# Products without a reader in two waits of TensorE: the first norm, and before the first output projection

## What is computed

```python
def rms_norm(x, g):
    xf = x.astype(jnp.float32)
    y = xf * lax.rsqrt(jnp.mean(xf * xf, axis=-1, keepdims=True) + EPS)
    return (y * g.astype(jnp.float32)).astype(x.dtype)
...
        x = x + mixers[i % N_MIXERS](rms_norm(x, norm_mix), *mix_params)
        x = x + sqrelu_mlp(rms_norm(x, norm_ffn), w1, w2)
```

## Time and profile before

| | us |
|---|---|
| median of 3 runs | 1702.68 |
| lowest, highest | 1695.72, 1703.55 |
| the profiled execution | 1700.87 |
| its span | 1698.8 |
| TensorE busy | 1627.7 (96%) |
| VectorE busy | 975.7 (57%) |
| ScalarE busy | 686.7 (40%) |
| mean granted clock of TensorE | 0.981 |

### The profile page before, as it was taken

The page is one execution under the profiler, slowest core; times in us unless marked ns, Lnnn a source line. Parts: engine busy times, 40 slices in busy tenths (PEclk is TensorE's granted clock), DMA queues, the critical chain, the costliest instruction groups (busy, mean ns, idle before and its releaser), DMA issues.

```text
span 1698.8 us, 24770 instructions
## 1 busy us (share of the span) xinstructions
PE 1627.7 (96%) x9418; PEld 1304.7 (77%) x9418; DVE 975.7 (57%) x1500; ACT 686.7 (40%) x1040; POOL 242.0 (14%) x222
## 2 busy tenths in 40 slices
PE   6999978999999999999799999999999999999998
PEld 3777757888888887667457888878787788888887
DVE  5555645444444457787466768586774544444443
ACT  6455543323232355424455445362543432323232
POOL 0234330000000033143200403104040000000000
PEclk7999989999999999999899999999999999999999
DMA  4222213333333334223103122131220333333333
GB/s 132 74 72 65 63 38 87 87 99 99 99 92 101 92 98 119 63 66 86 37 4 108 40 75 75 51 87 51 65 62 26 88 104 93 99 95 102 87 100 99
DMA packets 258158, 135.07 MB, mean 80 GB/s; under 512 B 10699, under 2 KB 254940, under 8 KB 258068
## 3 DMA queue, kind: packets, MB, share of 16 engines
q1 hardware_dynamic: 258068, 133.84, 28.1%
HBM read 131.64 MB, written 2.18 MB: 79 GB/s over the span
## 4 chain that ended last, share of the span: by engine, by line
PE 78%; DVE 9%; issue 7%; ACT 4%; POOL 1%; DMA 0%; DVEq 0%; POOLq 0%; PEldq 0%; ACTq 0%; SPq 0%; PEld 0%
PE bank L231 18%; PE bank L233 18%; PE bank L232 18%; PE bank L1680 4%; PE bank L493 3%; PE bank L495 3%; PE bank L494 3%; DVE arena L1985 2%; DVE w_lo L215 2%; ACT w_hi L211 1%; PE bank L1260 1%; PE bank L1514 1%; PE bank L1696 1%; PE bank L1733 1%; DVE arena L2127 1%
## 5 line engine op out<-in xcount | busy, mean ns | idle before, releaser
L211 ACT CAST w_hi<-raw 128x1024 fp32r<-128x1024 f32 x234 | 245.0, 1047 | 260.4 <-PE bank L233 237.3
L231 PE MATMUL bank<-m_hi,w_hi 128*128 128x512 f32 x856 | 337.5, 394 | 6.0 <-POOL w_lo L221 2.8
L233 PE MATMUL bank<-m_hi,w_lo 128*128 128x512 f32 x856 | 334.3, 391 | 0.0
L232 PE MATMUL bank<-m_lo,w_hi 128*128 128x512 f32 x856 | 334.3, 391 | 0.0
L215 DVE TENSOR_TENSOR w_lo<-raw,w_hi 128x1024 fp32r<-128x1024 f32 x218 | 271.2, 1244 | 102.4 <-ACT w_hi L211 100.6
L231 PE MATMUL bank<-h_hi,w_hi 128*128 128x512 f32 x640 | 256.2, 400 | 10.6 <-DVE w_lo L215 6.2
L232 PE MATMUL bank<-h_lo,w_hi 128*128 128x512 f32 x640 | 252.7, 395 | 0.0
L233 PE MATMUL bank<-h_hi,w_lo 128*128 128x512 f32 x640 | 252.4, 394 | 0.0
L231 PEld LDWEIGHTS bank<-m_hi,w_hi 128*128 128x128 f32 x856 | 161.5, 189 | 43.1 <-issue 5.5
L232 PEld LDWEIGHTS bank<-m_lo,w_hi 128*128 128x128 f32 x856 | 161.5, 189 | 34.4 <-issue 1.2
L233 PEld LDWEIGHTS bank<-m_hi,w_lo 128*128 128x128 f32 x856 | 161.4, 189 | 33.9
(11 more groups left out here) (282 smaller groups left out, 2264.4 us busy)
## 6 DMA issues: line engine op xcount, KB each, us to landing
raw<-in_l_w_ff SPq DMA_DIRECT2D x64, 512.0 KB, 4.0
raw<-in_w_in SPq DMA_DIRECT2D x64, 512.0 KB, 3.8
raw<-in_w_mlp_up SPq DMA_DIRECT2D x32, 512.0 KB, 4.0
raw<-in_w_mlp_down SPq DMA_DIRECT2D x32, 512.0 KB, 4.0
raw<-in_l_w_in SPq DMA_DIRECT2D x24, 512.0 KB, 3.8
raw<-in_l_w_out SPq DMA_DIRECT2D x8, 512.0 KB, 3.7
arena<-gb_rows SPq DMA_DIRECT2D x16, 256.0 KB, 4.7
raw<-in_w_out SPq DMA_DIRECT2D x8, 512.0 KB, 4.1
```

The source lines that it names most:

```text
L211: act.copy(w_hi[q.par][:], raw[q.par][:]).then_inc(s["w_hi_ready"], 1)
L231: pe.matmul(g_bank[q.par][:], w_hi[q.par][:, k], hi[:, k], start=(k == 0), stop=False)
L232: pe.matmul(g_bank[q.par][:], w_hi[q.par][:, k], lo[:, k], start=False, stop=False)
L233: last = pe.matmul(g_bank[q.par][:], w_lo[q.par][:, k], hi[:, k], start=False, stop=(k == KT - 1))
```

## The change

A helper issues n products into bank `b[5]`, whose results nothing reads. It is called in three places: five products ahead of the waits for `x_s` and `n_acc` in `pe_norm`, nine behind the product L380 and ahead of the fence, and eighteen behind the last head and ahead of the wait for `gla_done` and the second fence. The first fourteen take `ones` and the first 512 columns of `x_tok`, both plain f32; the eighteen take a tile of `w_hi` and one of `m_hi`, both f32r. No wait and no semaphore is added.

```diff
--- before.py
+++ after.py
@@ -373,11 +373,18 @@
                     low(k - 1)
             low(KT - 1)
 
+        def pe_keep_clock(pe, bk, left, right, n):
+
+            for i in range(n):
+                pe.matmul(bk[:], left, right, start=True, stop=True)
+
         def pe_norm(pe):
             pe.wait_ge(s["memsets"], 2)
+            pe_keep_clock(pe, b[5], ones[:], x_tok[:, 0, 0:SEQ], 5)
             pe.wait_ge(s["x_s"], KT)
             pe.wait_ge(s["n_acc"], KT)
             pe.matmul(b[0][:], ones[:], x_acc, start=True, stop=True).then_inc(s["n_ss"], 1)
+            pe_keep_clock(pe, b[5], ones[:], x_tok[:, 0, 0:SEQ], 9)
 
 
         at[0] = 0
@@ -589,6 +596,8 @@
                 part(22, 23)
 
             gla_heads(pe, body)
+            q = Panel(N_WO0, 0, 0, 0)
+            pe_keep_clock(pe, b[5], w_hi[q.par][:, 0], m_hi[:, 0], 18)
 
         def act_gla(act):
             def q_evac(g, e, u, q):
```

## The result

| | before | after |
|---|---|---|
| median, us | 1700.27 (9 runs) | 1711.51 (9 runs) |
| lowest to highest, us | 1694.83 to 1704.61 | 1703.49 to 1712.37 |
| the profiled execution, us | 1700.87 | 1703.49 |
| its mean granted clock | 0.981 | 0.990 |

The ratio of after to before is 1.0059, 95% interval [1.0041, 1.0078]: the change makes the kernel 10.0 us slower (7.0 to 13.3). The forecast was +9.8 us, 1710.7 us, with a range from 1706 to 1716.

The account below looks back on a forecast made before the run. The prediction took the path through TensorE's drain, which holds the first norm, to set the end. Norm 8.3, gate products 1.0, second place 0 and colder panel 0.5 gave +9.8 us on 1700.87: 1710.7 us, range 1706 to 1716.

Parts of the forecast that it names:

- The nine and the drain: First norm: the logarithm waits for TensorE's drain behind the nine products; 7.7 us of the 8.3 us delay.
- The price of 0.86 us: Both norm places: each added plain f32 product takes 0.86 us at full clock, with 0.27 us latency added once.
- The five: Ahead of L380: L380 starts 17.75 instead of 16.24 but runs at full clock; part of +8.3 us.
- The gate panel gains nothing from a warm clock: Gate panel behind the first norm: VectorE paces it at 1.39 us per k at either clock; gain nothing.
- The gate products: The four products L433 behind the gate panel: between -1.2 and +2.2 us by their clock, taken as +1.0 us.
- The second place costs and gains nothing; the clears pace the addition: Eighteen products behind the last head: cost 0, gain 0; VectorE's first addition to x waits for 39 clears.
- The colder panel behind it: Panel after the output projection: longer TensorE idling, 5.1 instead of 2.35 us; -1.7 to +1.8 us, taken as +0.5.
- Rival (a): First norm: clock falls at 14.8 us while the five run; 1.7 to 3.1 us more, 1712.4 to 1713.8; chance 0.13.
- (b): First norm: all fillers run at half clock, 25.8 us; +21 us, 1722; chance 0.04.
- (d): First norm: a product's two records overlap, fillers take 0.43 us instead of 0.86; +3.8 us, 1704.7; chance 0.06.
- (c): First norm: drain doesn't hold ScalarE for the nine, only the five cost; -2.3 to near +2 us; chance 0.07.
- The sum: Whole kernel: 8.3 + 1.0 + 0 + 0.5 = +9.8 us, giving 1710.7 us; range 1706 to 1716.

Follow-up runs that it names:

- second run: Kernel before plus only the five products ahead of L380: ratio 1.0008 [0.9995, 1.0021].
- fourth run: Kernel before plus only the nine products, moved behind the first fence and ahead of the gate panel, reading x: ratio 1.0005 [0.9992, 1.0017].
- third: Kernel before plus only the eighteen f32r products behind the last head: ratio 1.0002 [0.9992, 1.0012].
- fifth: Kernel before plus only thirty-six f32r products, instead of eighteen, behind the last head: ratio 1.0035 [1.0022, 1.0048], +6.0 us.
- sixth: Kernel before without added products, VectorE's 39 semaphore clears moved behind its part of the output projection: ratio 0.9979 [0.9967, 0.9991].
- seventh: Kernel before with the 39 clears moved behind VectorE's part of the projection, plus the eighteen products behind the last head: ratio 0.9983 [0.9972, 0.9995].
- tenth run: Kernel before plus the ninth kernel's edits, three products ahead of L380 and four behind the first fence: ratio 0.9988 [0.9972, 1.0004].
- eighth run: Kernel before plus only the nine products ahead of the first fence, in f32r form over the first panel's w_hi: ratio 1.0013 [0.9998, 1.0027].
- ninth kernel: Kernel before with clears moved, the eighteen products, and twelve more f32r products ahead of the next panel: ratio 0.9984 [0.9967, 1.0002].
- the last two: The ninth kernel and the tenth run, each against the kernel before: ratios 0.9984 and 0.9988.

## Why the prediction was right

**The nine and the drain** (8.3 us forecast with the five). 8.15 us in the trace after; 8.4 us with the nine alone; back at nothing with the same nine behind the fence. This was the decisive step, and it stood on two rows, and the earlier trace rows. The price of 0.86 us held (4.48 us for five with latency, 7.89 for nine).

**The five** (part of the 8.3). +0.5 us at the logarithm by the second run, +0.6 expected.

**The gate panel gains nothing from a warm clock.** Right. From the logarithm to the copy of the panel's result it is 13.75 to 13.77 us in the 11 traces in which the panel starts 3.7 to 3.8 us behind the logarithm, with its first k at either clock. Only the fourth run's, where it starts 8.9 us behind it, is longer.

**The gate products** (+1.0 us). In the trace after they took 4.45 us, not more than the 4.87 of before, so the term had the wrong sign there. That the kernel before was rather lucky was right: with the first place unchanged they took 5.61, 5.74 and 5.28 us in the third, fifth and sixth runs' traces, and 3.67 to 5.74 over all kernels here. The term wasn't needed.

**The second place costs and gains nothing; the clears pace the addition.** Right to 0.01 us in the trace after and with the eighteen alone. That the clears were the cover is shown by the sixth and seventh runs: without them TensorE is the releaser, and the twelve warm products are worth 1.3 us.

**The colder panel behind it** (+0.5 us). In the trace after, the stretch at half clock was 3.4 us again and the panel's eight k took 7.05 us, not 7.14, so nothing was added. With the eighteen alone it was 6.8 us and 7.65: the 0.5 us, as forecast. Which of the two is the rule stays open.

**Rival (a), the clock drops under the fillers**, did not come in the trace after. But the reason that I gave against it doesn't hold there, and that part was luck. I took the full clock "because it was 1.00 through the transposes"; in the trace after all transposes of x ran at half clock, and the clock rose at 14.1 us, 0.35 us ahead of the first filler. In the kernel before, too, they had run at 1.00 only from 7.9 us, not for over 8 us. In the second and the tenth run the reason held: the clock was up from 9.4 and 9.2 us, and stayed up through the fillers. In the fourth and the eighth run it fell at 11.4 and 11.9 us in the midst of the transposes, behind 1.7 and 1.3 us of waiting for the input (the rows at 10.24 and 11.66 above); five fillers behind those would have begun at half clock. How often that happens I haven't measured. The Trainium skill ("TensorE: Matmul & The Clock Gate", Part 4: PE-mode transpose) says of transposes that the full clock "doesn't engage" and that they don't count as busy "the same way". The traces here don't agree: in all 12 the clock rose when TensorE had done nothing but transposes. **(b)** and **(d)** fall by the 0.86 us, **(c)** by the logarithm's 10.45 us of waiting for the drain.

**The sum.** The range held. That 9.8 came so close to the 10.0 measured is in part luck: in the trace after the two places come to 8.15 - 0.4 for the gate products - 0.1 behind the second place, 7.6 us. The other 2.4 us no trace shows in place; they are within the interval (7.0 to 13.3), which also leaves open on which side of the forecast's 0.5% the change lies.

## What to carry to other kernels

Before filling a wait with work, look at what stands behind it in the engine's order: a product that nobody reads cost its full price here where a drain followed it before the others were let go, and nothing that the total shows one line further down. Price the filler by its own form (plain f32 was 3.8 times f32r here), and check that the work which is to run warm is what someone waits for; where another engine paces it, remove what makes that engine late first. Here 39 semaphore clears, moved out of the way, gave 0.9979 by themselves, and no filler added to that gave more. And before a clock column is trusted at the start of a trace, look at the pace of equal instructions there.

## What the runs showed that I had not expected

Two executions of one kernel can differ by some 10 us, in step with the mean granted clock: the kernel before went from 1694.71 to 1704.58 us in the 23 runs beside the last two, its mean clock from 0.985 to 0.979; the ninth kernel went from 1691.02 to 1700.74, its mean clock from 0.988 to 0.983. When the input comes differs too, by up to 0.8 us in the traces here. One profiled execution of each kernel therefore says little about the total (1703.49 and 1700.87 here, for medians 11 us apart), while distances between neighbouring instructions agreed to 0.01 us.

Moving the clears gave 3.6 us (1.5 to 5.6) by the total for 0.5 us in place. The one trace has 1.55 us more in the panel behind, which ran warm; that the shorter idling ahead of it is the cause is argued, not shown, and the rest of the 3.6 us is not seen in that trace.
